# A whole output tile ahead of the pairs, squares a step later and joins ahead of the low halves, in a hybrid pooling and attention layer on one core

## The chip, the core and the metric

The kernel runs on one core of a Trainium2 chip. The engines are TensorE (PE, its weight loads PEld), VectorE (DVE), ScalarE (ACT), GpSimd (POOL) and SyncE (SP). SP and POOL only issue transfers in the part that matters here. The metric is the device time of one execution in microseconds (us). The time before is a median of 853.5 us.

## The reference, cut to what matters

The layer takes 512 prompt rows and 8 sample rows (520 columns once turned), projects them, runs pooling and attention branches, and ends with an output projection, a residual and a final RMS norm. The change touches only this last part.

```
def merge_out(pm, gp, a, ga, w_out, dtype):
    mix = jnp.concatenate([pm * silu(gp), a * silu(ga)], axis=-1)      # 520 x 2048
    return jnp.einsum('btm,md->btd', mix, w_out)                        # w_out is 2048 x 2048
...
xp = xp + merge_out(...)
y_prompt = rms_norm(xp, final_norm_g)     # y * rsqrt(mean(y*y) + 1e-6) * g
```

## The kernel before, in words

All products are made of three fp32 matmuls: each operand is split in a high half (ScalarE copies it to `..._hi`) and a low half (VectorE subtracts: `..._lo`), and TensorE sums high by high, high by low and low by high. A column block of `w_out`, 128 wide, is an output tile `d`, 16 of them. Each takes 16 blocks of 128 rows of `w_out` (`k`).

The work is written as a list of steps, the same for each engine, and each engine runs its own part of every step in turn. 144 steps belong to the input projection. Those of the output are counted here from 0 (`n`).

- **Whole tiles.** Tiles 0, 1 and 2 are woven: steps 0 to 8 run their three chunks (6, 5 and 5 `k`) in turn, into the banks `pj[0]`, `pj[1]` and `ps_s`/`ps_o`. A chunk is loaded three steps ahead by SP (`load_chunk`) into one of three slots of `w_raw`, split two steps ahead (`split_hi`, line 1130, and `split_lo`, line 1559), and used by `chunk` (line 864).
- **Pairs.** Tiles 3 to 12 go in five pairs ("duos"), six steps each, numbered k = 0 to 5 here. A pair uses sums of halves of the weights and of the inputs so that its first eight `k` take seven products instead of eight. Its units are w11, s1, s2, s3, w12, s4, w22 (12 matmuls each) and std1x, std1y, std2x, std2y for the other eight `k` (24 each): 180 matmuls of 260 columns, all on line 1022. The std2y unit of a pair runs in step 0 of the next. Weights go through a ring of six places in `w_hi`, `w_lo` and `parts` (`unit_hi_of`, line 1354, `unit_lo_of`, lines 2080 and 2084); VectorE makes the weight sums s1 to s4 (`weight_sum`, line 2105).
- **Joins.** ScalarE takes snapshots of partial sums from PSUM (`snapshot`, line 1366, and `take_c21`, line 1372). VectorE adds a bank and a snapshot (`meet`, line 2112, "join" here), three in step 5 and one in step 1 of the next pair, and turns the finished tile (`turn_both`, lines 2119 and 2120). w11 of the next pair waits for the second join of step 5.
- **The trip of a tile.** After the turn, POOL stores the tile to a scratch in DRAM in four transfers (`send_tile`, line 1532), SP loads it back as rows (`load_rows`, line 637), VectorE adds the residual (`add_res`, lines 2018 and 2021), ScalarE squares it for the norm (`y_square`, line 1325, five instructions with their accumulator reads) and VectorE scales it by `g` (`scale_y`, lines 2030 and 2031). SP then loads the residual of tile d + 3 into the freed buffer (`load_res`, line 644).
- **Input sums for the pairs.** VectorE makes them in steps 2 to 7 (`whole_x`, `form_sums`, `form_lo_of`), ScalarE their high halves in steps 5 and 6.
- **The end.** Tile 13 (`SOLO`) is a whole tile after the pairs. Tiles 14 and 15 are last: columns 256 to 519 as halves (`half_chunk`, line 890), taken by `half_evict` (line 1314) and turned on TensorE (`turn_half`), then rows 0 to 255 directly (`row_chunk`, line 901). `half_add`, `half_square`, `root` and `scale_last` finish the norm and SP stores the rows.

In ScalarE's list of a step the order is snapshots of `duo_early`, high halves, snapshots of `duo_late`, then squares. In VectorE's list it is

```
if IN_CHUNKS + SEVEN - 2 <= step < IN_CHUNKS + AFTER:
    for p, u in units_ahead(step):
        unit_lo_of(p, u)
    duo_sums(step)
if duo_at(step):
    duo_out(*duo_at(step))
```

Of the kernel before, what the change touches and what calls it, by code (L numbers as in the profile page):

```python
# [28 lines left out]
KT = D_MODEL // P  # L29
# [29 lines left out]
SEVEN = WOVEN * 3  # L59
DUO_STEPS = 6  # L60
AFTER = SEVEN + DUOS * DUO_STEPS
SOLO = WOVEN + 2 * DUOS
OUT_SEQ = tuple((d, c) for c in range(3) for d in range(WOVEN)) + tuple(
    (d, c) for d in range(SOLO, KT) for c in range(3))
# [76 lines left out]
def layer_step(nc, x_prompt, x_sample, state_pool, cache_k, cache_v, norm_g, w_in, pool_w,  # L141
               pool_scale, w_out, final_g, consts, y_prompt, y_sample, pool_state_p, k_win_p,
               v_win_p, pool_state_s, k_new, v_new):
    with ExitStack() as ctx:
# [299 lines left out]
        def split_ahead(step):  # L444

            n = step - IN_CHUNKS
            if n <= SEVEN - 3 or n >= AFTER + 1:
                return (chunk_at(step + 2),) if n < OUT_CHUNKS - 2 else ()
            return {AFTER - 1: (chunk_at(step + 1),),
                    AFTER: (chunk_at(step + 1), chunk_at(step + 2))}.get(n, ())  # L450
# [24 lines left out]
        TAIL = IN_CHUNKS + SEVEN + 3  # L475
# [20 lines left out]
        def w_both(c):  # L496

            lo, hi = TAIL_CHUNKS[c]
            if c == 0:
                flat = [a.rearrange("p j x -> p (j x)") for a in (pt_hi, pt_lo)]  # L500
            elif c == 1:
                flat = [a[:, 0:2].rearrange("p s k x -> p (s k x)") for a in (w_hi, w_lo)]
            else:
                flat = [a.rearrange("p j x -> p (j x)") for a in (v_hl, pooled_lo)]
            return tuple(a[:, 0:HP * (hi - lo)].rearrange("p (k x) -> p k x", k=hi - lo)
                         for a in flat)

        def out_bank(d):

            return (ps_s, ps_o) if d in (2, SOLO) else pj[d % 2 if d < 2 else (d + 1) % 2]  # L510
# [5 lines left out]
        def done_at(d):  # L516

            if d < WOVEN:
                return IN_CHUNKS + OUT_N[d, 2]
            if d >= SOLO:  # L520
                return IN_CHUNKS + 3 * d + 2
            p, second = divmod(d - WOVEN, 2)
            return IN_CHUNKS + SEVEN + DUO_STEPS * p + (7 if second else 4)

        def rows_at(d):

            return done_at(d) + (5 if d < WOVEN else 4)

        def added_at(d):

            return done_at(d) + (7 if d < WOVEN else 5)

        def duo_banks(p):

            a, b = (pj[0][0], pj[1][0]) if p % 2 == 0 else (pj[1][0], pj[0][0])
            return {"a": a, "b": b, "c": pj[0][1], "d": pj[1][1]}
# [14 lines left out]
        def _(sp):  # L551

            def load_chunk(n):
# [102 lines left out]
            def load_duo(p, what):  # L656

                m1, m2 = WOVEN + 2 * p, WOVEN + 2 * p + 1
# [28 lines left out]
            for step in range(STEPS):  # L687
                if step + 3 < IN_CHUNKS + SEVEN:
                    load_chunk(step + 3)
                elif step == IN_CHUNKS + AFTER - 2:  # L690
                    load_chunk(IN_CHUNKS + SEVEN)
                elif step == IN_CHUNKS + AFTER - 1:
                    load_chunk(IN_CHUNKS + SEVEN + 1)
                    load_chunk(IN_CHUNKS + SEVEN + 2)
                elif step == IN_CHUNKS + AFTER:
                    load_chunk(IN_CHUNKS + SEVEN + 3)
# [40 lines left out]
                if n == 4:  # L737
                    load_duo(0, "c")
                if n == 5:
# [3 lines left out]
                if n == 7:  # L743
# [3 lines left out]
                if n == 10:  # L747
# [3 lines left out]
                if n in (11, 12):  # L751
                    load_res(n - 10)
                if n >= 0:
# [3 lines left out]
                    for e in range(3, KT):  # L757
                        if step == added_at(e - 3) + 2:
                            sp.wait_ge(y_scaled, e - 2)
                            load_res(e)  # L760
            for e in range(3, KT):
                if added_at(e - 3) + 2 >= STEPS:
# [34 lines left out]
        def _(pe):  # L797
# [28 lines left out]
            def chunk(n):  # L826
# [6 lines left out]
                else:  # L833
# [6 lines left out]
                    elif c == 0:  # L840
                        pe.wait_ge(yt_done, WOVEN)
# [200 lines left out]
            def duo_step(p, k):  # L1042

                if k == 0:
                    if p < DUOS:
                        pe.wait_ge(*((yt_done, 1) if p == 0 else (met, 4 * p - 2)))
# [10 lines left out]
                if k == 2:  # L1057
                    pe.wait_ge(*((yt_done, 2) if p == 0 else (c21_out, p)))
# [53 lines left out]
        def _(act):  # L1112
            def split_hi(n):
# [4 lines left out]
                if n >= TAIL and c == 1:  # L1118
                    act.wait_ge(w_used, TAIL)
                elif n == IN_CHUNKS + SEVEN:  # L1120
                    act.wait_ge(unit_used, RING_N[DUOS - 1, "w12"] + 1)
                elif n == IN_CHUNKS + SEVEN + 1:
                    act.wait_ge(unit_used, RING_N[DUOS - 1, "s4"] + 1)
                elif n == IN_CHUNKS + SEVEN + 2:
                    act.wait_ge(unit_used, RING_N[DUOS - 1, "w22"] + 1)
                elif n == TAIL:
                    act.wait_ge(unit_used, len(RING_SEQ))
# [240 lines left out]
            def take_c21(p):  # L1368

                act.wait_ge(unit_used, RING_N[p, "std2y"] + 1)  # L1370
                act.wait_ge(yt_done, WOVEN + 2 * p + 1)
# [19 lines left out]
            for step in range(STEPS):  # L1391
# [41 lines left out]
                if n == 5:  # L1433
                    form_hi_of("nt1")
                    form_hi_of("t3")
                if n == 6:
# [103 lines left out]
        def _(dve):  # L1540
# [467 lines left out]
            def add_res(d):  # L2008
# [8 lines left out]
                op = ALU.subtract if WOVEN <= d < SOLO and (d - WOVEN) % 2 == 1 else ALU.add  # L2017
# [113 lines left out]
            def duo_out(p, k):  # L2131
# [4 lines left out]
                if k == 2 and p > 0:  # L2136
                    dve.wait_ge(met, 4 * p)
                    dve.wait_ge(c21_out, p)
                    turn_both(WOVEN + 2 * p - 1)
                if k == 5 and p < DUOS:  # L2140
# [5 lines left out]
                    turn_both(WOVEN + 2 * p)  # L2146

            for step in range(STEPS):
                for pr, j, p in due(step):
                    early(pr, j, p)  # L2150
                if step > 0:
                    for m in split_ahead(step):
                        split_lo(m)
                if IN_CHUNKS + SEVEN - 2 <= step < IN_CHUNKS + AFTER:
# [3 lines left out]
                if duo_at(step):  # L2158
                    duo_out(*duo_at(step))
                for d in range(KT - 2):  # L2160
                    if step == done_at(d) + 1 and (d < WOVEN or d >= SOLO):
# [28 lines left out]
                if n in (2, 3):  # L2190
                    whole_x(n - 2)
                if n in (4, 5):
                    form_sums(n - 4)
                if n == 6:
                    form_lo_of("nt1")
                    form_lo_of("t3")
                if n == 7:
                    form_lo_of("nt2")
                    form_lo_of("t4")
                for d in range(KT - 2):  # L2200
                    if step == added_at(d) + 1:
# [120 lines left out]
```

## Time and profile before

| | us |
|---|---|
| median of three runs | 853.5 |
| lowest, highest | 852.5, 856.26 |
| the profiled execution's own time | 853.96 |
| its span, first to last instruction | 852.2 |
| mean granted TensorE clock, share of full speed | 0.988 |

The profiled execution is 1.8 us longer than its span and 0.5 us above the median. TensorE is busy 830.2 us of the span. The page's slices show it at nine tenths or more of each slice except in three of the last seven of forty, and the input projection (to about 655 us) is no part of the change. What follows reads the stretch from 680 us to the end.

### The profile page before, as it was taken

Reading aid. Unit: us, or ns where it says so; the run is one execution under the profiler, and the core shown is the slowest. Engines: PE = TensorE matmul, PEld = TensorE weight load, DVE = VectorE, ACT = ScalarE, POOL = GpSimd, SP = SyncE. Lnnn points to the kernel's source line nnn. Section 1 sums busy time; section 2 is a strip of 40 time slices with the busy share of each in tenths; the row PEclk is TensorE's granted clock in tenths of the full one; section 3 lists DMA queues with packets and bytes.
Section 4 is the critical chain, followed back from the end, with each engine's and each line's share of the span. In section 5 each row is a group of like instructions: output and inputs, shape, how many; then the busy total and the mean of one; then the engine's idle time right before and its main releaser. Section 6 shows DMA issues by size and latency. Waiting matters only on the chain.

```text
span 852.2 us, 17454 instructions
## 1 busy us (share of the span) xinstructions
PE 830.2 (97%) x6765; PEld 823.3 (97%) x6765; DVE 608.0 (71%) x1305; ACT 395.2 (46%) x875; POOL 98.3 (12%) x172
## 2 busy tenths in 40 slices
PE   9999999999999999999999999999999998999985
PEld 8999999999999999999999999999999988999975
DVE  5646884797579568757975796688788967767445
ACT  5745535423543454255435434643463545555443
POOL 2001000201010001002000101010001032222220
PEclk9999999999999999999999999999999998999988
DMA  8566347537544752564366347534768375565645
GB/s 286 151 169 163 91 121 176 131 105 177 147 110 117 193 141 78 167 173 111 93 173 165 98 134 196 150 89 129 182 187 299 96 219 157 157 181 154 198 117 202
DMA packets 247307, 131.69 MB, mean 155 GB/s; under 512 B 40864, under 2 KB 239968, under 8 KB 247200
## 3 DMA queue, kind: packets, MB, share of 16 engines
q1 hardware_dynamic: 239928, 119.17, 51.3%
q0 software_dynamic: 7296, 11.40, 4.3%
q8 instruction: 54, 0.88, 0.5%
q14 instruction: 29, 0.24, 0.1%
HBM read 110.32 MB, written 19.10 MB: 152 GB/s over the span
## 4 chain that ended last, share of the span: by engine, by line
PE 86%; DVE 5%; DMA 3%; ACT 2%; issue 1%; SPq 1%; POOL 0%; DVEq 0%; ACTq 0%
PE pj L864 66%; PE pj L1022 9%; PE ps_t L908 2%; PE ps_o L952 1%; PE ps_s L923 1%; PE ps_s L921 1%; DMA arena<-in_x_prompt 1%; PE ps_o L950 1%; ACT arena L1325 1%; PE ps_s L969 1%; PE ps_t L969 1%; PE pj L890 1%; DVE w_lo L2084 1%; PE ps_o L864 0%; PE ps_s L864 0%
## 5 line engine op out<-in xcount | busy, mean ns | idle before, releaser
L864 PE MATMUL pj<-mov_hi,w_hi 128*128 128x260 f32 (+1 forms) x1600 | 328.6, 287 | 0.3 <-DVE mov_lo L1580 0.3
L864 PE MATMUL pj<-mov_hi,w_lo 128*128 128x260 f32 (+1 forms) x1600 | 322.1, 283 | 0.0
L864 PE MATMUL pj<-mov_lo,w_hi 128*128 128x260 f32 (+1 forms) x1600 | 321.3, 282 | 0.0
L864 PEld LDWEIGHTS pj<-mov_hi,w_hi 128*128 128x128 f32 x1600 | 246.4, 189 | 0.9 <-issue 0.7
L864 PEld LDWEIGHTS pj<-mov_lo,w_hi 128*128 128x128 f32 x1600 | 246.4, 188 | 0.0
L864 PEld LDWEIGHTS pj<-mov_hi,w_lo 128*128 128x128 f32 x1600 | 246.4, 188 | 0.0
L1130 ACT ACTIVATE w_hi<-w_raw 128x640 fp32r<-128x640 f32 (+1 forms) x157 | 121.4, 773 | 209.4 <-PE pj L864 176.7
L1559 DVE TENSOR_TENSOR w_lo<-w_raw,w_hi 128x640 fp32r<-128x640 f32 (+1 forms) x157 | 136.0, 866 | 63.3 <-ACT w_hi L1130 63.0
L1190 ACT ACTIVATE parts<-ps_t 128x128 fp32r<-128x128 f32 (+1 forms) x64 | 26.2, 436 | 80.4 <-PE ps_t L908 78.5
L1650 DVE TENSOR_TENSOR parts<-ps_t,parts 128x128 fp32r<-128x128 f32 (+1 forms) x64 | 29.7, 485 | 45.8 <-ACT parts L1190 45.6
L1532 POOL DMA_DIRECT2D y_scratch<-arena x56 | 37.5, 677 | 120.6 <-DVE arena L2120 95.1
L1022 PE MATMUL pj<-mov_hi,w_hi 128*128 128x260 f32 x144 | 41.8, 290 | 5.4 <-DVE arena L2112 2.8
L1597 DVE SCALAR_TENSOR_TENSOR arena<-pj,rstd_bc 128x260 f32<-128x260 f32 (+2 forms) x104 | 36.9, 399 | 13.0 <-PE pj L864 11.2
L1174 ACT ACTIVATE arena<-arena,stat 128x128 f32<-128x128 f32 (+1 forms) x64 | 35.7, 558 | 17.4 <-DVE stat L1636 16.8
L1022 PE MATMUL pj<-mov_hi,w_lo 128*128 128x260 f32 x144 | 41.5, 288 | 0.0
L1022 PE MATMUL pj<-mov_lo,w_hi 128*128 128x260 f32 x144 | 41.5, 288 | 0.0
L1636 DVE CUSTOM_DVE_ANT_0 arena<-ps_s,arena 128x128 f32<-128x128 f32 (+1 forms) x64 | 29.7, 482 | 16.4 <-PE ps_s L923 16.4
L1182 ACT ACTIVATE arena<-arena,stat 128x128 f32<-128x128 f32 (+1 forms) x64 | 34.2, 558 | 14.7 <-DVE stat L1644 14.6
L1325 ACT ACTIVATE arena<-arena 128x128 f32<-128x128 f32 (+1 forms) x70 | 21.7, 310 | 34.0 <-DVE arena L2021 32.2
L1022 PEld LDWEIGHTS pj<-mov_hi,w_hi 128*128 128x128 f32 x144 | 27.9, 193 | 6.2 <-DVE arena L2112 3.3
L1490 POOL DMA_DIRECT2D out<-arena x8 | 4.5, 568 | 243.4 <-DMA arena<-arena 243.4
L1022 PE MATMUL pj<-mov_hi,parts 128*128 128x260 f32 x152 | 30.2, 291 | 0.1
(271 smaller groups left out, 1331.2 us busy)
## 6 DMA issues: line engine op xcount, KB each, us to landing
w_raw<-in_w_in SPq DMA_DIRECT2D x96, 320.0 KB, 3.6
w_raw<-in_w_in SPq DMA_DIRECT2D x48, 384.0 KB, 3.8
arena<-in_cache_k_win SPq DMA_DIRECT2D x16, 384.0 KB
arena<-in_cache_v_win SPq DMA_DIRECT2D x16, 384.0 KB
w_raw<-in_w_out SPq DMA_DIRECT2D x26, 192.0 KB, 3.4
arena<-in_cache_k_win SPq DMA_DIRECT2D x8, 512.0 KB
arena<-in_cache_v_win SPq DMA_DIRECT2D x8, 512.0 KB
arena<-in_x_prompt SPq DMA_DIRECT2D x16, 256.0 KB
```

The costliest lines, as they stand in the source:

```text
L864: mm = pe.matmul(dst[h][:, 0:own.stop - own.start], w, m[:, k, own], start=(k == 0 and i == 0), stop=(c == 2 and k == KT - 1 and i == 2))
L1022: mm = pe.matmul(dst, w[:, own], m(k), start=(at in first and k == 0 and i == 0), stop=(at in last and k == KQ - 1 and i == 2), skip_group ...
L1130: act.activation(w_at(n)[0][:, 0:hi - lo, :], w_raw[:, n % SLOTS, 0:hi - lo, :], ACT.Copy).then_inc(w_hi_done, 1)
L1174: act.activation(pb_, pb_, ACT.Exp, scale=-1.0, bias=nmax[:, i:i + 1], accum_out=den[:, i:i + 1]).then_inc(exped, 1)
L1182: a = act.activation(pb_, pb_, ACT.Copy, scale=rden[:, i:i + 1])
L1190: a = act.activation(pt_hi[:, 0:i + 1, P * i:P * i + P], ps_t[:, at:at + P * (i + 1)].rearrange("p (j x) -> p j x", j=i + 1), ACT.Copy)
L1325: act.activation(sq_junk[0:n, :], src, ACT.Square, accum_out=ss_y[0:n, t, d:d + 1]).then_inc(y_squared, 1)
L1532: pool.dma_start(rows[:, :, own], y_sq[d % 3][own, :].rearrange("p (c x) -> p c x", x=SQ)).then_inc(y_st[d % 3], 16)
L1559: dve.tensor_tensor(to_lo[:, 0:hi - lo, :], w_raw[:, n % SLOTS, 0:hi - lo, :], to_hi[:, 0:hi - lo, :].bitcast(F32), ALU.subtract).then_inc ...
L1597: o = dve.scalar_tensor_tensor(out=dst, in0=pj[a][h][:, c0:c1], scalar=scale, in1=rstd_bc[:, HT * h + c0:HT * h + c1], op0=ALU.mult, op1=A ...
L1636: dve.tensor_tensor_reduce(out=pbuf[r % 2][:, at:at + n], in0=ps_s[:, at:at + n], in1=nbias[:, SEQ - n:SEQ], scale=1.0, scalar=3e38, op0=A ...
L1650: o = dve.tensor_tensor(pt_lo[blk], ps_t[:, at:at + P * (i + 1)].rearrange("p (j x) -> p j x", j=i + 1), pt_hi[blk].bitcast(F32), ALU.subt ...
```

## The change

Tile 3 becomes a whole tile and runs in steps 9 to 11, right after the woven ones, into bank `pj[0]`. The five pairs now make tiles 4 to 13 in steps 12 to 41, and nothing whole is left after them: the last six chunks (tiles 14 and 15) follow at once, and their weights go to places of `parts` that the first pair units leave. The number of matmuls, of split and of stored elements is the same.

```
-SEVEN = WOVEN * 3
+FIRST = WOVEN + 1
+SEVEN = FIRST * 3
...
 OUT_SEQ = tuple((d, c) for c in range(3) for d in range(WOVEN)) + tuple(
-    (d, c) for d in range(SOLO, KT) for c in range(3))
+    (d, c) for d in (WOVEN, KT - 2, KT - 1) for c in range(3))
...
-        TAIL = IN_CHUNKS + SEVEN + 3
+        TAIL = IN_CHUNKS + SEVEN
...
         def rows_at(d):
-            return done_at(d) + (5 if d < WOVEN else 4)
+            return min(done_at(d) + (6 if d < FIRST else 4), STEPS - 2)
         def added_at(d):
-            return done_at(d) + (7 if d < WOVEN else 5)
+            return min(done_at(d) + (8 if d < FIRST else 6), STEPS - 1)
+        def squared_at(d):
+            return min(added_at(d) + 1, STEPS - 1)
+        def scaled_at(d):
+            return min(squared_at(d) + 1, STEPS - 1)
...
-                if n == IN_CHUNKS + SEVEN:
-                    sp.wait_ge(unit_lo, RING_N[DUOS - 1, "std2x"] + 1)
-                elif n == IN_CHUNKS + SEVEN + 1:
-                    sp.wait_ge(unit_lo, RING_N[DUOS - 1, "std2y"] + 1)
+                if TAIL <= n < TAIL + SLOTS:
+                    last = ("std2x", "std2y", "s4")[n - TAIL]
+                    sp.wait_ge(unit_lo, RING_N[DUOS - 1, last] + 1)
...
                 elif step == IN_CHUNKS + AFTER - 2:
-                    load_chunk(IN_CHUNKS + SEVEN)
+                    load_chunk(TAIL)
+                    load_chunk(TAIL + 2)
                 elif step == IN_CHUNKS + AFTER - 1:
-                    load_chunk(IN_CHUNKS + SEVEN + 1)
-                    load_chunk(IN_CHUNKS + SEVEN + 2)
+                    load_chunk(TAIL + 1)
...
-                if n >= TAIL and c == 1:
-                    act.wait_ge(w_used, TAIL)
...
+                if n >= TAIL:
+                    act.wait_ge(unit_used, RING_N[DUOS - 1, "s4" if c == 1 else "s3"] + 1)
...
                 for d in range(KT - 2):
-                    if step == added_at(d):
+                    if step == squared_at(d):
                         y_square(d)
...
+                if duo_at(step):
+                    duo_out(*duo_at(step))
                 if IN_CHUNKS + SEVEN - 2 <= step < IN_CHUNKS + AFTER:
                     for p, u in units_ahead(step):
                         unit_lo_of(p, u)
                     duo_sums(step)
-                if duo_at(step):
-                    duo_out(*duo_at(step))
...
-                if n in (2, 3):
-                    whole_x(n - 2)
+                if n in (3, 4):
+                    whole_x(n - 3)
```

The input sums move one step later, their halves two. Of a pair's two tiles, the first is added in step 4 and squared in step 5 (before: both in step 3), the second added in step 1 and squared in step 2 (before: both in step 0).

ScalarE in a pair in the middle, before, from step 3 to step 1 of the next: `L1325` are squares, `tab<-pj` is the snapshot s3, `rstd_bc<-pj` the snapshot w11, `L1372` is `take_c21`, `L1354` are high halves.

```order
L1325 ACTIVATE arena<-arena 128x128 x4
L1325 ACTIVATE arena<-arena 8x128
L1366 ACTIVATE tab<-pj 128x260
L1354 ACTIVATE w_hi<-tab 128x512
L1354 ACTIVATE w_hi<-w_raw 128x512 x2
L1354 ACTIVATE parts<-w_raw 128x512 x2
L1366 ACTIVATE rstd_bc<-pj 128x260
L1325 ACTIVATE arena<-arena 128x128 x4
L1325 ACTIVATE arena<-arena 8x128
L1372 ACTIVATE arena<-pj 128x260
```

The same engine and place in the changed kernel, where every line number of ScalarE is 5 lower:

```order
L1361 ACTIVATE tab<-pj 128x260
L1349 ACTIVATE w_hi<-tab 128x512
L1349 ACTIVATE w_hi<-w_raw 128x512 x2
L1320 ACTIVATE arena<-arena 128x128 x4
L1320 ACTIVATE arena<-arena 8x128
L1349 ACTIVATE parts<-w_raw 128x512 x2
L1361 ACTIVATE rstd_bc<-pj 128x260
L1367 ACTIVATE arena<-pj 128x260
```

Squares no longer stand ahead of the snapshot s3 or of `take_c21`; they stand behind the high halves of step 5 (and, not shown, of step 2).

VectorE before, in the steps 4 and 5 of a pair: `w_raw<-tab,extra` is the sum s1 of the next pair, `L2030` and `L2031` scale a tile, then the low half and the sum, then the joins (`L2112`) and the turn.

```order
L2084 TENSOR_TENSOR w_lo<-tab,w_hi 128x512
L2080 SCALAR_TENSOR_TENSOR w_lo<-w_raw,w_hi 128x512
L2105 TENSOR_TENSOR w_raw<-tab,extra 128x512
L2030 TENSOR_TENSOR arena<-arena 128x4x128
L2031 TENSOR_TENSOR arena<-arena 8x128
L2084 TENSOR_TENSOR w_lo<-w_raw,w_hi 128x512
L2105 TENSOR_TENSOR w_raw<-w_raw,tab 128x512
L2112 TENSOR_TENSOR tab<-rstd_bc,tab 128x260
L2112 TENSOR_TENSOR arena<-pj,rstd_bc 128x260
```

The same engine and place in the changed kernel; `L2013` and `L2016` are `add_res`:

```order
L2079 TENSOR_TENSOR w_lo<-tab,w_hi 128x512
L2075 SCALAR_TENSOR_TENSOR w_lo<-w_raw,w_hi 128x512
L2100 TENSOR_TENSOR w_raw<-tab,extra 128x512
L2013 TENSOR_TENSOR arena<-arena 128x4x128
L2016 TENSOR_TENSOR arena<-arena 8x128
L2107 TENSOR_TENSOR tab<-rstd_bc,tab 128x260
L2107 TENSOR_TENSOR arena<-pj,rstd_bc 128x260
L2107 TENSOR_TENSOR arena<-pj,extra 128x260
L2114 STREAM_TRANSPOSE arena<-arena 128x512
L2115 STREAM_TRANSPOSE arena<-arena 128x32
L2079 TENSOR_TENSOR w_lo<-w_raw,w_hi 128x512
```

The low half of s1 and the sum s2 now follow the joins and the turn, and an `add_res` stands where the scaling stood.

ScalarE at the end, before, from the first square behind the chunks to the second taking (`L1314` is `half_evict`):

```order
L1130 ACTIVATE parts<-w_raw 128x4x128
L1325 ACTIVATE arena<-arena 128x128 x4
L1325 ACTIVATE arena<-arena 8x128
L1314 ACTIVATE arena<-pj 128x264
L1325 ACTIVATE arena<-arena 128x128 x4
L1325 ACTIVATE arena<-arena 8x128
L1314 ACTIVATE arena<-pj 128x264
```

The same engine and place in the changed kernel:

```order
L1125 ACTIVATE parts<-w_raw 128x4x128
L1309 ACTIVATE arena<-pj 128x264
L1320 ACTIVATE arena<-arena 128x128 x4
L1320 ACTIVATE arena<-arena 8x128
L1320 ACTIVATE arena<-arena 128x128 x4
L1320 ACTIVATE arena<-arena 8x128
L1309 ACTIVATE arena<-pj 128x264
```

The taking of tile 14 now stands ahead of both last squares (tiles 12 and 13), that of tile 15 behind both.

## Rows read from the trace of the kernel before

**Rows 1.** The page's first part: busy time of each engine and its share.

```profile
PE 830.2 (97%) x6765; PEld 823.3 (97%) x6765; DVE 608.0 (71%) x1305; ACT 395.2 (46%) x875; POOL 98.3 (12%) x172
```

**Rows 2.** Windows of TensorE: stretch, length, busy (count), granted clock, DMA share, GB/s.

```profile
684.00:688.00 4.00, 3.20 (x25) 1.00 0.27 56
701.00:710.00 9.00, 6.21 (x39) 0.81 0.51 132
713.00:720.00 7.00, 4.83 (x28) 0.76 0.67 184
819.00:824.00 5.00, 0.89 (x8) 0.81 0.34 96
824.00:829.00 5.00, 5.00 (x24) 0.51 0.24 68
```

**Rows 3.** Timeline of TensorE: start, length, instruction: first matmul of pairs, tile 13, tile 14.

```profile
681.84 0.28 PE L1022 MATMUL pj<-mov_hi,parts 128*128 128x260 f32 x1
800.07 0.28 PE L864 MATMUL ps_s<-mov_hi,w_hi 128*128 128x256 f32 x1
811.59 0.28 PE L890 MATMUL pj<-mov_hi,parts 128*128 128x264 f32 x1
```

**Rows 4.** The chain in order of time from 728 us: start, length, what.

```profile
727.93 41.49 PE pj L1022 x346
```

**Rows 5.** Timeline in the first pair: VectorE and ScalarE; brackets: idle before, releaser.

```profile
698.38 0.69 DVE L2105 TENSOR_TENSOR w_raw<-tab,extra 128x512 f32<-128x512 f32 x1 [1.34 <-DMA extra<-in_w_out]
698.98 0.68 DVE L2018 TENSOR_TENSOR arena<-arena 128x512 f32<-128x512 f32 x1
699.89 0.31 ACT L1325 ACTIVATE arena<-arena 128x128 f32<-128x128 f32 x1 [3.67 <-DVE arena L2021]
702.59 0.69 DVE L2084 TENSOR_TENSOR parts<-w_raw,parts 128x512 fp32r<-128x512 f32 x1 [2.73 <-ACT parts L1354]
704.26 0.42 DVE L2112 TENSOR_TENSOR arena<-pj,rstd_bc 128x260 f32<-128x260 f32 x1
```

**Rows 6.** The same timelines, in the third and fourth pair.

```profile
744.36 0.69 DVE L2018 TENSOR_TENSOR arena<-arena 128x512 f32<-128x512 f32 x1 [0.80 <-DMA arena<-y_scratch]
745.28 0.31 ACT L1325 ACTIVATE arena<-arena 128x128 f32<-128x128 f32 x1 [2.50 <-DVE arena L2021]
748.24 0.69 DVE L2084 TENSOR_TENSOR w_lo<-tab,w_hi 128x512 fp32r<-128x512 f32 x1 [3.00 <-ACT w_hi L1354]
766.58 0.69 DVE L2018 TENSOR_TENSOR arena<-arena 128x512 f32<-128x512 f32 x1 [0.79 <-DMA arena<-y_scratch]
```

**Rows 7.** The same at the end, with POOL, SP and TensorE.

```profile
802.18 0.83 ACT L1130 ACTIVATE parts<-w_raw 128x768 fp32r<-128x768 f32 x1
809.12 0.96 DVE L1559 TENSOR_TENSOR w_lo<-w_raw,w_hi 128x768 fp32r<-128x768 f32 x1 [4.00 <-ACT w_hi L1130]
810.00 0.70 DVE L2119 STREAM_TRANSPOSE arena<-arena 128x512 f32<-128x512 f32 x1
811.09 5.34 POOL L1532 DMA_DIRECT2D y_scratch<-arena x8 [12.09 <-DVE arena L2120]
816.27 0.38 SPq L637 DMA_DIRECT2D arena<-y_scratch  x1
820.47 0.69 DVE L2018 TENSOR_TENSOR arena<-arena 128x512 f32<-128x512 f32 x1 [2.13 <-DMA arena<-y_scratch]
823.43 0.36 ACT L1314 ACTIVATE arena<-pj 128x264 f32<-128x264 f32 x1
823.85 0.69 PE L908 MATMUL ps_t<-tab,arena 128*128 128x128 f32 x2 [4.11 <-ACT arena L1314]
824.63 0.39 SPq L644 DMA_DIRECT2D arena<-in_x_prompt  x1
832.82 0.42 DVE L2210 TENSOR_TENSOR arena<-ps_s,arena 128x256 f32<-128x256 f32 x1 [5.40 <-PE ps_o L908]
841.75 0.28 PE L901 MATMUL pj<-parts,mov_hi 128*128 128x256 f32 x1
842.71 0.48 DVE L2220 TENSOR_TENSOR arena<-pj,arena 128x128 f32<-128x128 f32 x2
```

**Rows 8.** The page's DMA issues: destination<-source, queue, operation, count, KB each, median us to landing.

```profile
w_raw<-in_w_in SPq DMA_DIRECT2D x48, 384.0 KB, 3.8
w_raw<-in_w_out SPq DMA_DIRECT2D x26, 192.0 KB, 3.4
```

More of the change, by code:

```diff
@@ L448, in split_ahead @@
                 return (chunk_at(step + 2),) if n < OUT_CHUNKS - 2 else ()
-            return {AFTER - 1: (chunk_at(step + 1),),
-                    AFTER: (chunk_at(step + 1), chunk_at(step + 2))}.get(n, ())
+            return {AFTER - 1: (TAIL,), AFTER: (TAIL + 1, TAIL + 2)}.get(n, ())
         def units_ahead(step):
@@ L498, in w_both @@
             lo, hi = TAIL_CHUNKS[c]
-            if c == 0:
-                flat = [a.rearrange("p j x -> p (j x)") for a in (pt_hi, pt_lo)]
-            elif c == 1:
+            if c == 1:
                 flat = [a[:, 0:2].rearrange("p s k x -> p (s k x)") for a in (w_hi, w_lo)]
             else:
-                flat = [a.rearrange("p j x -> p (j x)") for a in (v_hl, pooled_lo)]
+                at = 0 if c == 0 else HP * 6
+                flat = [parts[:, at + h:at + h + HP * 6] for h in (0, len(FORMS) * WING)]
             return tuple(a[:, 0:HP * (hi - lo)].rearrange("p (k x) -> p k x", k=hi - lo)
@@ L736, in _ @@
                     load_split(i)
-                if n == 4:
+                if n == SEVEN - 5:
                     load_duo(0, "c")
-                if n == 5:
+                if n == SEVEN - 4:
                     sp.wait_ge(own_done, PAIRS)
@@ L750, in _ @@
                     load_res(0)
-                if n in (11, 12):
-                    load_res(n - 10)
+                if n in (SEVEN, SEVEN + 1):
+                    load_res(n - SEVEN + 1)
                 if n >= 0:
@@ L757, in _ @@
                     for e in range(3, KT):
-                        if step == added_at(e - 3) + 2:
+                        if step == scaled_at(e - 3) + 1:
                             sp.wait_ge(y_scaled, e - 2)
@@ L2016, in add_res @@
                 cols = slice(P * d, P * d + P)
-                op = ALU.subtract if WOVEN <= d < SOLO and (d - WOVEN) % 2 == 1 else ALU.add
+                op = ALU.subtract if d >= FIRST and (d - FIRST) % 2 == 1 else ALU.add
                 dve.tensor_tensor(y[:, :, cols],
@@ L2157, in _ @@
                     duo_sums(step)
-                if duo_at(step):
-                    duo_out(*duo_at(step))
                 for d in range(KT - 2):
-                    if step == done_at(d) + 1 and (d < WOVEN or d >= SOLO):
+                    if step == done_at(d) + 1 and d < FIRST:
                         turn_out(d)
@@ L2200, in _ @@
                 for d in range(KT - 2):
-                    if step == added_at(d) + 1:
+                    if step == scaled_at(d):
                         scale_y(d)
```

55 lines of the change are left out of this document (22 added, 33 removed).

## The prediction

> **What bounds the kernel now.** Start with the page's first part: TensorE is busy for 97% of the span and no other engine for more than 71% [rows 1], so only TensorE's idle or slow time can be won, plus what lies behind its last matmul. The windows of TensorE in the changed stretch come next. It is short of work in four places [rows 2]: a little at 684 us, then 2.8 us idle from 701 and 2.2 us from 713, both followed by a granted clock of half speed, and at 819 us, where 4.1 us idle is again followed by half speed.
>
> How much the pairs lose is best read over their whole length. They run from the first matmul of w11 at 681.84 to the first of tile 13 at 800.07 [rows 3], 118.2 us for 5 x 180 = 900 matmuls. In the dense stretch of the chain 346 matmuls take 41.49 us [rows 4], 0.1199 each, so 900 need 107.9. **The pairs lose 10.3 us.** The windows agree: idle 0.8 + 2.8 + 2.2 = 5.8, slow clock (1 - 0.81) x 9 + (1 - 0.76) x 7 = 3.4, together 9.2 [rows 2]; the rest is what the windows hide, since a matmul is 0.28 long and one starts every 0.12 [rows 3, 4], so 0.16 of each gap counts as busy.
>
> Why they lose it is read from the timelines of VectorE and ScalarE. VectorE's sum s1 waits 1.34 us for a transfer at 698.38, the residual add stands behind it, ScalarE can square only from 699.89, and the high half that VectorE wants for s1 stands behind those squares: VectorE idles 2.73 us before 702.59. The join that lets the next w11 go is behind all this, at 704.26 [rows 5]. So TensorE waits for a chain that is late because the first pair starts with its helpers already behind. Later pairs show a second, milder thing: squares at 745.28 (behind an add that waited 0.80 us for its rows) hold the snapshot s3 and the halves behind it, so VectorE idles 3.00 us before 748.24. The adds follow one another at 744.36 and 766.58, 22.2 us apart [rows 6], though 180 matmuls need only 21.6. TensorE, coming late out of the first two pairs, hardly feels this loop; it would on time.
>
> At the end, VectorE's low half waits 4.00 us before 809.12, because its high half waits for tile 13's second chunk on TensorE; the turn of tile 12 stands behind it at 810.00. Its trip ends in an add at 820.47, squares, the taking at 823.43 and TensorE's turning at 823.85 [rows 7]. That is the 4.1 us.
>
> **Part by part.** *The whole tile ahead of the pairs.* It costs TensorE nothing net, 96 matmuls either way (811.59 - 800.07 = 11.5 us [rows 3]). For the helpers it is cover: in those 11.5 us VectorE gets three low halves of at most 0.96 and a turn of about 0.9 (as one of 0.70 plus a short one) [rows 7], 3.8 in all, and ScalarE three high halves, under 3. So VectorE gains 7.7 us on TensorE before the first pair, ScalarE over 8. The three waits that the first two pairs showed sum to 5.8 us idle, and these are lateness that adds up along one chain; 7.7 covers it with 1.9 to spare. The input sums one step later and their halves two steps later stay ahead: a step is 3.6 us or more, and the first use moved three steps. SP's loads for the first pairs and three residual loads, which now crowd the transfers (one of them is what s1 waited for at 698.38), move with the steps and get the same 11.5 us. That the moved loads cost anything is bounded by the 1.34 us of that wait, below the cover, so I take nothing.
>
> *Squares a step later.* Off ScalarE's path from unit s3 to the next join come five squares of about 2.1 us (699.89 to the high half behind them, [rows 5]). New positions are behind high halves that TensorE needs only two units later. From the end of s3, snapshot, two high halves, low half, sum s1, add and two joins are 0.4 + 1.1 + 0.7 + 0.7 + 0.9 + 0.8 = 4.6 us (durations as in rows 5 to 7), while TensorE has w12, s4, w22 and std2x ahead of w11, 60 matmuls or 7.2 us. Slack 2.6 us. What is late next is nothing in a pair; the y rows now have a full step more, and the trip of 10.5 us (810.00 to 820.47, [rows 7]) fits in the 18 us between turn and add. The loop of 22.2 us opens.
>
> *Joins ahead of the low halves.* The join c waits for s4 on TensorE, and s1's low half of the next pair is queued behind three joins and a turn, about 1.9 us. TensorE wants it after w22, std2x, w11 and std2y, 72 matmuls or 8.6 us after s4. Cost nothing, with 6.7 us of cover.
>
> So the pairs should run at 21.6 us each and **end at 681.84 + 11.5 + 107.9 = 801.3** against 811.6 for the same work. Up to 0.3 us of small waits may remain.
>
> *The end.* The halves of tile 14 now start at 801.3. Their chunks are ready: the first's slot is free when the last std2x low half is, some 12 us earlier, the second's and third's some 8 us earlier. What is left is the last tile's trip, which has lost the cover of tile 13:
> - std2y ends at 801.3, snapshot 0.4, high half 0.85, low half 0.9, join 0.35, add 0.9, low half 0.9: turn of tile 13 starts at about 805.6;
> - add at 805.6 + 10.5 = 816.1 (810.00 to 820.47), end 817.0;
> - squares and taking: 823.85 - 821.35 = 2.5 from the end of the add to the turning, so 819.5 [rows 7]; the add of 820.47 ends 0.9 later.
>
> TensorE meanwhile does 48 + 18 matmuls, a turning that is ready in time, 30, and 18 of the first row chunk: 114 x 0.1199 + 0.4 = 14.1, to 815.4. It **waits 4.1 us again**, until 819.5, and falls to half speed as at 824 (lost (1 - 0.51) x 5 = 2.4). Then 78 matmuls: 0.7 + 9.4 + 2.4, last one at 832.0. Before, the last was at 841.75 + 0.3 [rows 7]. So TensorE ends 10.1 us sooner at least; before, VectorE picked it up 0.7 us late (842.71), which it need not now. On VectorE, the residual load of tile 15 goes out after the scaling of tile 12 at about 817.9 (before: 824.63) and lands within the 4.2 us that rows take (816.27 to 820.47), 822.1; `half_add` then, against 832.82, is 10.7 sooner, and its last row add at 832.0 too. Both paths meet at 832.0, where 842.71 was. **Gain 10.7 us.**
>
> A row and the skill differ here. Between the end of POOL's first four issues (811.09 + 2.67 = 813.76) and SP's load at 816.27 lie 2.5 us [rows 7]. The Trainium skill, "DMA: Bandwidth & Descriptors", section "Anatomy of one DMA — SWDGE (gpsimd) path", gives about 2.0 us fixed plus bytes / 436e3, which for 68 KB is an estimate of 2.2 us. By it the trip would be 0.3 us shorter and the gain 11.0.
>
> The sum is made on the span of 852.2, which becomes 841.5; the profiled run is 1.8 longer than its span and 0.5 above the median, so against the median of 853.5 the forecast is **842.8 us**.
>
> **Rivals.**
> - *The end is worse than counted.* The second store of two took longer to be picked up than the first, and the rows' load ranges over a microsecond; with a second stretch of half speed like that from 824 to 829 (2.4) and the trip 1.2 longer, the time is 844.5 to 846.5. For it: everything there is serial now. Against: only about 1 us of it is unpriced.
> - *The loop of 22.2 us stays.* If SP's queue, not the squares, sets it, each pair costs 0.6 us more: 842.8 + 3.1 = 845.9. For: the add waits for rows in both pairs [rows 6]. Against: the add now stands a step later.
> - *Half of the first stall stays.* If the first pairs are late for transfers and not for VectorE, the 2.8 us idle with its 1.7 of slow clock returns: 847.3.
> - *The end is better.* If the last tile's trip is short by 1.5 us, 841.3; less is barred by VectorE's own list behind `half_add`.
> - *The change doesn't do what it says:* the pairs are dense but the end takes all back. The half tiles use a chunk in 18 matmuls, 2.2 us, where tile 13 took 4.3. With three slots, a load (3.8 us, [rows 8]), a high half (0.83) and a low half (0.96, [rows 7]) give one chunk in 1.9 us, just faster. If loads went one at a time, three chunks at 5.6 us each would cost 3 x 3.4 = 10.2: 853.0, no change.
> - *Slower.* The joins ahead of the low halves turn into the bound: a join waits for TensorE (s4), the low half behind it, TensorE for that. It starts to cost once the low half comes more than 8.6 us after s4 instead of 1.9, and outweighs the gain at 2.1 us more per pair (10.7 / 5). With 3.5 us per pair the time is 842.8 + 17.5 = 860.3. Nothing in the rows is near it.
>
> **How the numbers follow.** Forecast 842.8, own range 841.3 to 844.5: 0.58. Worse end 0.14, loop 0.10, half a stall 0.07, better end 0.05; no change 0.03; slower 0.03. A measurement of this kernel can tell about 0.5% (4.3 us) from no change: faster means under 849.2. The first five cases are there, 0.94; same 0.03; slower 0.03. The range takes the forecast's own and reaches over the worse end and the loop: 841.0 to 846.8, leaving out the half stall and what lies beyond, and part of the better end.
>
> **What would show it.** In the windows of the changed kernel, TensorE without idle time and at full clock from 655 us to about 815 us; the first pair's matmuls from 693.4 and tile 14's from 801.3. In the timelines, no squares between s3's snapshot and the next join, adds 21.6 us apart. At the end, one wait of TensorE of about 4 us before the turning for tile 15, caused by ScalarE's taking behind the squares of tile 13, then half speed. The prediction is wrong if TensorE waits in `duo_step` for a low half, a join or the bank of tile 3, if the half tiles wait for chunks, or if the last wait is far from 4 us.

## The result, and the profile after

The changed kernel takes **840.24 us** (median of 4 runs, 839.13 to 842.67) against 853.4 of the kernel before: a ratio of 0.9844, 95% interval 0.9812 to 0.9876. That is 13.2 us less where 10.7 were forecast. The forecast of 842.8 was 2.6 us too slow, and the fast end of its range, 841.0, was too slow by 0.8; the ratio's interval, which is 837.4 to 842.8 us, reaches over that end of the range. The profiled run has a span of 838.1 us where the sum came to 841.5.

The windows of TensorE (stretch, length, busy (count), granted clock, DMA share, GB/s), after, against [rows 2]:

```profile
684.00:688.00 4.00, 4.00 (x36) 1.00 0.44 99
701.00:710.00 9.00, 9.00 (x77) 1.00 0.58 166
713.00:720.00 7.00, 7.00 (x61) 1.00 0.70 189
815.00:820.00 5.00, 2.95 (x15) 0.73 0.23 66
820.00:825.00 5.00, 5.00 (x41) 0.93 0.27 100
```

The three places of the pairs have closed. The chain of waits after (start, length, what) shows the pairs in one piece, and then the end:

```profile
681.52 11.53 PE pj L867 x96
693.05 107.75 PE pj L1025 x900
...
804.93 0.62 DVE arena L2114
...
808.39 2.13 DMA y_scratch<-arena
810.53 0.36 SPq L640
810.94 2.71 DMA arena<-y_scratch
813.67 0.69 DVE arena L2013
...
814.56 0.60 DVE arena L2025
...
815.39 0.37 SPq L647
815.81 0.41 SPq L649
816.26 2.92 DMA arena<-in_final_norm_g
819.28 0.42 DVE arena L2205
```

900 matmuls of the pairs take 107.75 us, where 107.9 was the forecast. Behind them TensorE no longer stands in the chain that ended last. The chain goes by the turn of tile 13 (804.93), its stores, its rows' load, its add (813.67), the scaling of tile 12 (814.56), the three transfers of the residual load of tile 15 (the last is the row of `g`) and `half_add` (819.28).

TensorE's own wait at the end is there, at the place that was forecast, but half as long:

```profile
816.64 0.36 ACT L1309 ACTIVATE arena<-pj 128x264 f32<-128x264 f32 x1
817.05 0.53 PE L911 MATMUL ps_s<-tab,arena 128*128 128x128 f32 x2 [2.17 <-ACT arena L1309]
828.08 0.28 PE L904 MATMUL pj<-parts,mov_hi 128*128 128x256 f32 x1
829.18 0.48 DVE L2215 TENSOR_TENSOR arena<-pj,arena 128x128 f32<-128x128 f32 x2
```

Since runs reach the changed stretch at 659.5 to 661.8 us, kernels are compared below by three lengths, read from TensorE's timeline. P runs from the matmul right behind the last product of the mixing (660.15 before, 659.67 after) to the first of tile 14: the same matmuls in every kernel, 140.95 us at their best. T runs from there to TensorE's last matmul, E from there to the span's end. All three come from the one profiled run of each kernel. Of the 14.1 us between the spans before and after, P has 10.5, T 2.7, E 0.4 and the earlier arrival 0.5.

| kernel | median us | ratio (95% interval) | P | T | E |
|---|---|---|---|---|---|
| before | 853.4 | 1 | 151.4 | 30.2 | 10.4 |
| after | 840.24 | 0.9844 (0.9812 to 0.9876) | 141.0 | 27.4 | 10.0 |
| e3_tile_only | 847.06 | 0.9907 (0.9886 to 0.9928) | 147.6 | 27.0 | 10.6 |
| e1_squares_back | 850.95 | 0.9953 (0.9939 to 0.9968) | 150.8 | 26.6 | 10.6 |
| e2_joins_back | 840.91 | 0.9839 (0.9814 to 0.9864) | 141.0 | 27.4 | 9.2 |
| e4_no_tile | 841.85 | 0.9851 (0.9829 to 0.9874) | 142.5 | 26.2 | 10.6 |
| n1_squares_only | 841.92 | 0.9853 (0.9836 to 0.9871) | 142.2 | 27.2 | 10.3 |
| n2_adds_back | 843.64 | 0.9877 (0.9862 to 0.9892) | 141.0 | 29.3 | 10.4 |
| n3_same_step | 846.78 | 0.9907 (0.9890 to 0.9925) | 142.0 | 29.6 | 10.7 |
| t1_store_traffic | 841.26 | 0.9850 (0.9836 to 0.9865) | 141.0 | 27.0 | 10.3 |
| v1_take_first | 839.89 | 0.9840 (0.9827 to 0.9854) | 141.0 | 23.6 | 12.7 |
| v2_scale_first | 838.98 | 0.9830 (0.9816 to 0.9843) | 141.0 | 26.0 | 10.4 |
| v3_both | 837.49 | 0.9808 (0.9795 to 0.9822) | 141.0 | 23.6 | 11.7 |

The kernel before, measured again beside each group of runs, had medians of 853.4 (after), 854.79 (e), 854.42 (n) and 853.66 (t and v). So a difference of about 1 us between medians of different groups says nothing; the ratios take it out.

### The profile page after: what moved, and what is told of

Read it like the earlier page. It is cut to its first block, busy times and chain, and to the rows that moved or that the text cites. A ratio compares the mean times of both kernels' runs of the same rounds, so it can differ in the third digit from the quotient of the medians.

```text
span 838.1 us, 17458 instructions
## 1 busy us (share of the span) xinstructions
PE 822.6 (98%) x6765; PEld 817.0 (97%) x6765; DVE 608.5 (73%) x1305; ACT 395.8 (47%) x875; POOL 98.3 (12%) x172
## 4 chain that ended last, share of the span: by engine, by line
PE 94%; DMA 2%; DVE 1%; SPq 1%; ACT 1%; issue 0%; POOL 0%; DVEq 0%; ACTq 0%
PE pj L867 70%; PE pj L1025 13%; PE ps_t L911 2%; PE ps_o L955 1%; PE ps_s L926 1%; PE ps_s L924 1%; DMA arena<-in_x_prompt 1%; PE ps_o L953 1%; PE ps_o L867 1%; PE ps_t L972 1%; PE ps_s L972 1%; PE ps_s L867 1%; PE ps_m L911 0%; DMA arena<-in_final_norm_g 0%; DMA arena<-y_scratch 0%
## 5 line engine op out<-in xcount | busy, mean ns | idle before, releaser
L867 PE MATMUL pj<-mov_hi,w_hi 128*128 128x260 f32 (+1 forms) x1632 | 335.0, 287 | 0.6 <-DVE w_lo L1582 0.6
L867 PE MATMUL pj<-mov_hi,w_lo 128*128 128x260 f32 (+1 forms) x1632 | 328.6, 283 | 0.0
L867 PE MATMUL pj<-mov_lo,w_hi 128*128 128x260 f32 (+1 forms) x1632 | 327.8, 282 | 0.0
L867 PEld LDWEIGHTS pj<-mov_hi,w_hi 128*128 128x128 f32 x1632 | 251.3, 189 | 1.0 <-issue 0.7
L867 PEld LDWEIGHTS pj<-mov_lo,w_hi 128*128 128x128 f32 x1632 | 251.4, 188 | 0.0
L867 PEld LDWEIGHTS pj<-mov_hi,w_lo 128*128 128x128 f32 x1632 | 251.3, 188 | 0.0
L1185 ACT ACTIVATE parts<-ps_t 128x128 fp32r<-128x128 f32 (+1 forms) x64 | 26.2, 435 | 79.4 <-PE ps_t L911 77.2
L1592 DVE SCALAR_TENSOR_TENSOR arena<-pj,rstd_bc 128x260 f32<-128x260 f32 (+2 forms) x104 | 36.9, 400 | 12.2 <-PE pj L867 10.3
L1485 POOL DMA_DIRECT2D out<-arena x8 | 4.5, 567 | 244.4 <-DMA arena<-arena 244.4
L1705 DVE TENSOR_TENSOR arena<-arena 128x128 f32<-128x128 f32 (+3 forms) x48 | 28.8, 601 | 1.6
L1501 POOL DMA_DIRECT2D out<-arena x32 | 16.3, 510 | 100.4 <-DVE arena L1944 100.4
```

The source lines that it names most:

```text
L867: mm = pe.matmul(dst[h][:, 0:own.stop - own.start], w, m[:, k, own], start=(k == 0 and i == 0), stop=(c == 2 and k == KT - 1 and i == 2))
L1185: a = act.activation(pt_hi[:, 0:i + 1, P * i:P * i + P], ps_t[:, at:at + P * (i + 1)].rearrange("p (j x) -> p j x", j=i + 1), ACT.Copy)
L1592: o = dve.scalar_tensor_tensor(out=dst, in0=pj[a][h][:, c0:c1], scalar=scale, in1=rstd_bc[:, HT * h + c0:HT * h + c1], op0=ALU.mult, op1=A ...
L1705: o = dve.tensor_tensor(out, vv[:, P * to:P * (to + n)], vv[:, P * other:P * (other + n)], ALU.add)
```

## The experiments: which part closed the waits in the pairs

**The tile alone**, both smaller parts undone:

```diff
-            return min(done_at(d) + (6 if d < FIRST else 4), STEPS - 2)
+            return min(done_at(d) + (5 if d < FIRST else 4), STEPS - 2)
...
-            return min(done_at(d) + (8 if d < FIRST else 6), STEPS - 1)
+            return min(done_at(d) + (7 if d < FIRST else 5), STEPS - 1)
...
-            return min(added_at(d) + 1, STEPS - 1)
+            return added_at(d)
...
-                if duo_at(step):
-                    duo_out(*duo_at(step))
                 if IN_CHUNKS + SEVEN - 2 <= step < IN_CHUNKS + AFTER:
...
+                if duo_at(step):
+                    duo_out(*duo_at(step))
```

> The changed kernel with both smaller parts undone: only the whole tile stands ahead of the pairs. Theory of the prediction: the three waits of the first two pairs go (10.3 us less 3.3 for the loop of 22.2 us), 843.5. Rival: the tile alone does everything, 840.2 to 841. Second rival: the halves need both, and one of the first stalls comes back with its slow clock, 845 to 848.

Measured: 847.06, which is the second rival, and P = 147.6. The tile by itself is worth 3.8 of the 10.5 us. The largest stall is not covered: it has only moved, from ahead of the second pair to ahead of unit w22 of the first, which wants the taking of s3. In the kernel before it was this one:

```profile
704.74 0.39 PE L1022 MATMUL pj<-mov_hi,w_hi 128*128 128x260 f32 x1 [2.79 <-DVE arena L2112]
```

Timelines of VectorE, ScalarE and TensorE of the tile-only kernel:

```profile
697.74 0.68 DVE L2013 TENSOR_TENSOR arena<-arena 128x512 f32<-128x512 f32 x1
698.64 0.31 ACT L1320 ACTIVATE arena<-arena 128x128 f32<-128x128 f32 x1 [1.84 <-DVE arena L2016]
700.96 0.62 ACT L1349 ACTIVATE parts<-w_raw 128x512 fp32r<-128x512 f32 x1
701.61 0.69 DVE L2079 TENSOR_TENSOR parts<-w_raw,parts 128x512 fp32r<-128x512 f32 x1 [3.00 <-ACT parts L1349]
703.42 0.68 DVE L2013 TENSOR_TENSOR arena<-arena 128x512 f32<-128x512 f32 x1
704.33 0.31 ACT L1320 ACTIVATE arena<-arena 128x128 f32<-128x128 f32 x1 [1.72 <-DVE arena L2016]
706.38 0.62 ACT L1349 ACTIVATE w_hi<-w_raw 128x512 fp32r<-128x512 f32 x1
707.02 0.69 DVE L2075 SCALAR_TENSOR_TENSOR w_lo<-w_raw,w_hi 128x512 fp32r<-128x512 f32 x1 [1.92 <-ACT w_hi L1349]
707.63 0.68 DVE L2013 TENSOR_TENSOR arena<-arena 128x512 f32<-128x512 f32 x1
708.54 0.31 ACT L1320 ACTIVATE arena<-arena 128x128 f32<-128x128 f32 x1 [1.55 <-DVE arena L2016]
710.59 0.36 ACT L1361 ACTIVATE tab<-pj 128x260 f32<-128x260 f32 x1
711.00 0.51 PE L1025 MATMUL pj<-parts,w_hi 128*128 128x260 f32 x2 [3.13 <-ACT tab L1361]
```

Read it as a ring. VectorE's add of tile 0 (L2013) releases ScalarE's five squares (L1320, 2 us); the high half of the next step (L1349) stands behind them; VectorE's low half waits for it; the next tile's add stands behind the low half. A round takes 5.7 and 4.2 us, and both engines wait in it. Three tiles are added in a row here, and the taking of s3 (L1361), which TensorE wants, stands behind the third. The helpers had been in time: in the changed kernel and here alike, ScalarE waits 3.53 us for TensorE's w11 before its first taking, at 694.5 and 695.0. That the tile gave them no lead is read so: the next things in their lists are takings of what TensorE has yet to compute.

**The two smaller parts without the tile**: the kernel before with the changed kernel's steps of adds and squares and its order of the joins (the lines that the diff above takes out).

> The kernel before with the two smaller parts alone: adds a step and squares two steps later, joins ahead of the low halves, tile 13 still behind the pairs. Theory of the prediction: the first pair starts with its helpers late, so the waits of 2.8 and 2.2 us and the slow clock behind them stay: 851 to 853.5. Rival: VectorE's wait of 2.73 us at 702.59 was for squares, and the join behind it was what TensorE waited for, so these two parts take away most of the 10 us by themselves: 843 to 846.

Measured: 841.85. The theory of the prediction falls: without the tile P is 142.5, and all that is left of the waits are two of 0.6 us (by the starts of the matmuls) at 685 and 687 us. Beside the two smaller parts the tile is worth 1.5 us of P. The windows that lost most, at 701 and 713 us, close without the tile.

**The smaller parts one by one**: joins back (the last piece of that diff on the changed kernel), and squares back (its other pieces).

> The changed kernel with the joins behind the low halves and the sums again in each step of VectorE's list; the tile ahead and the late squares stay. Theory of the prediction: the joins have 6.7 us of cover either way, so the pairs stay at 107.7 us and the time at 840.2 within 1. Rival: a join behind a low half that waits for its high half holds the next w11 or std2x as at 704.26 in the kernel before, 0.6 us in each of 5 pairs: 843.2.

Measured: 840.91, P the same to a hundredth. The joins ahead of the low halves bring nothing that shows.

> The changed kernel with the adds and squares of the output rows back at their old steps (adds 5 or 7 steps after a tile's last unit, squares in the same step); the tile ahead of the pairs and the joins ahead of the low halves stay. Theory of the prediction: the squares in ScalarE's list set a loop of 22.2 us per pair, so the pairs take 5 x 22.2 = 111 instead of 107.7 us and the time is 840.2 + 3.3 = 843.5. Rival: the helpers come out of the extra tile some 7.7 us ahead, and a loop of 22.2 us eats only 0.6 of that per pair, 3 us in all, so TensorE never feels it and the time stays 840.2 within 1. Slower than 843.5 would mean that the squares also hold the first pair.

Measured: 850.95, slower than either theory had, and 3.9 us slower than the tile alone, from which it differs only in that the joins stand ahead of the low halves. It has the same stall in the first pair (3.29 us by the starts of the matmuls), and then one in each later pair. ScalarE, VectorE and TensorE of this kernel:

```profile
744.35 0.27 DVE L2016 TENSOR_TENSOR arena<-arena 8x128 f32<-8x128 f32 x1
744.66 0.31 ACT L1320 ACTIVATE arena<-arena 128x128 f32<-128x128 f32 x1 [1.96 <-DVE arena L2016]
746.71 0.36 ACT L1367 ACTIVATE arena<-pj 128x260 f32<-128x260 f32 x1
747.10 0.43 DVE L2107 TENSOR_TENSOR arena<-pj,tab 128x260 f32<-128x260 f32 x1 [2.48 <-ACT arena L1367]
747.62 0.69 DVE L2079 TENSOR_TENSOR w_lo<-w_raw,w_hi 128x512 fp32r<-128x512 f32 x1
748.47 0.36 PE L1025 MATMUL pj<-mov_hi,w_hi 128*128 128x260 f32 x1 [1.18 <-issue]
```

The join (L2107) waits 2.48 us for a taking (L1367) that stands behind squares, and the low half that TensorE starts with at 748.47 is now behind the join. This is the "slower" rival of the prediction in part: a low half stands behind a join. But this join is the one of step 1, which waits for `take_c21` behind squares and not for s4, and the price is smaller: about 1 us in a pair (waits of 0.5, 1.3, 1.7 and 1.1 us), and only while the squares are early.

**The late squares alone**, in the kernel before, and two runs that part "late" into its two steps:

> The kernel before with one part alone: adds a step and squares two steps later; no tile moved, joins behind the low halves. New theory: what TensorE waited for was a ring between two lists. ScalarE's squares stand in the step of VectorE's add and ahead of the next high halves; the next add stands behind the low halves that want these high halves. Each tile added in a row costs a round of 4.2 to 5.7 us where TensorE's step takes 3.6. Squares in a later step break the ring. Then this part alone gives nearly all: pairs at 109 us, 841.5 to 843. Rival: the joins ahead of the low halves do a share of it: 845 to 849.

Measured: 841.92, P = 142.2. One part of three, step numbers alone, gives 9.2 of the 10.5 us in P.

> The changed kernel with the adds back at their old step, the squares one step behind them. The ring's theory: it is the step between add and squares that counts, so the pairs stay dense: 840.2 within 1. Rival: what helps is that the adds wait for no rows any more (0.80 us before), and the ring comes back: 845 or more.

In code: `rows_at` and `added_at` with 5, and 7 or 5; `squared_at` stays `added_at + 1`. Measured: P = 141.0, so the pairs are as dense as with the adds late. The time is 843.64 all the same. T is 1.9 us longer and E 0.4; another 2.1 us of the profiled run is that it reached the stretch later. At the end, the high half of tile 14's second chunk comes at 806.70, so the turn of tile 13 starts 5.7 us behind the first matmul of tile 14 instead of 4.2, and TensorE waits 3.24 us before its last turning. The load of the chunk came last, not the squares ahead: ScalarE idles between them and the high half.

```profile
806.70 0.84 ACT L1125 ACTIVATE w_hi<-w_raw 128x768 fp32r<-128x768 f32 x1 [0.58 <-DMA w_raw<-in_w_out]
```

Here this load stands behind a residual load in SP's queue; in the changed kernel it went out ahead of it.

> The changed kernel with the squares in the step of the add again, both a step later than in the kernel before. The ring's theory: the ring is back, though every add comes later: a wait of about 3 us and a slow clock in the first pair, and the joins ahead of the low halves now wait for the takings behind the squares, about 1 us in every pair: 848 to 851. Rival: the later add is what helps: 840.2 to 841.5.

In code: `squared_at(d)` returns `added_at(d)`, with the late adds. Measured: P = 142.0, where the ring's theory wanted about 150. The span of the profiled run (844.79) is 4.9 us behind the changed kernel's: 2.2 in T, 1.0 in P, 0.7 in E and 1.1 of later arrival. The median of 846.78 is two us more, which the other runs have and no trace shows. So the theory needs a correction. The ring is back (squares behind adds at 702.12, 706.34 and 712.02), but only two of its rounds lie ahead of the taking of s3 instead of three:

```profile
708.38 0.36 ACT L1361 ACTIVATE tab<-pj 128x260 f32<-128x260 f32 x1
708.80 0.51 PE L1025 MATMUL pj<-parts,w_hi 128*128 128x260 f32 x2 [0.32 <-ACT tab L1361]
```

TensorE waits 0.32 us instead of 3.13. These rows show that a round of the ring costs about 4 us and that TensorE has slack for nearly two. The account that fits all runs is that either delay (of the add, or of the squares behind it) takes the third round out from in front of s3 and the squares away from the taking that the join wants. Both delays one by one were run only beside the whole tile and the early joins, not in the kernel before.

## The experiments: the end

The last tile's trip from turn to add was priced at 10.5 us by the kernel before. It takes 8.8 (804.86 to 813.67). The DMA issues (count, KB each, median us to landing) from 809 to 823 us in the kernel before, and of the same stores in the changed kernel:

```profile
y_scratch<-arena POOLq DMA_DIRECT2D x8, 68.0 KB, 3.1
...
w_raw<-in_w_out SPq DMA_DIRECT2D x1, 320.0 KB, 3.1
...
w_raw<-in_w_out SPq DMA_DIRECT2D x1, 192.0 KB, 3.8
w_raw<-in_w_out SPq DMA_DIRECT2D x2, 64.0 KB, 3.0
```

```profile
y_scratch<-arena POOLq DMA_DIRECT2D x4, 68.0 KB, 2.2
```

**Traffic put back.** In the changed kernel:

```diff
+                if d == KT - 3:
+                    sp.wait_ge(unit_used, len(RING_SEQ))
+                    sp.wait_ge(yt_done, KT - 2)
+                    for raw in (raw_a, raw_b, raw_c):
+                        sp.dma_start(raw.rearrange("p (k x) -> p k x", k=4),
+                                     wo[:, 0:4, 0:P]).then_inc(id_in, 16)
                 sp.wait_ge(y_st[d % 3], Y_ST * (d // 3 + 1))
```

> The changed kernel with three more loads of 256 KB each into tiles that nobody reads any more, issued by SP when the turned tile 13 goes to its stores, ahead of SP's wait for these stores. Theory A: the last tile's trip took 10.5 us in the kernel before and 8.8 us now because the stores shared the DMA engines with loads of weights (3.1 us to land against 2.2). Then the four stores land about 1 us later, the add of tile 13 comes at 10 us or more behind its turn, and the time is 1 to 2 us longer, 841.2 to 842.2. Rival B: stores behind one another in POOL's queue made the difference (eight in a row before, four now); then nothing moves, 840.2.

Measured: the stores land in 3.5 us, the rows' load goes out at 811.77, the add of tile 13 comes 9.9 us behind its turn, and TensorE waits 3.23 us:

```profile
806.86 1.33 POOL y_scratch L1533 x2
808.19 3.57 DMA y_scratch<-arena
811.77 0.37 SPq L646
...
814.54 0.69 DVE arena L2019
```

The last DMA of the chain is 3.57 us long instead of 2.13 (the changed kernel's chain, above). Theory A holds for the stores, which explains 1.1 us of the 1.7. From the start of the last store to SP's load of the rows are 3.2 us in the kernel before, 2.1 in the changed one and 3.6 here; from that load to the add 4.2, 3.1 and 2.8. So this run put the stores back in company and not the rows' load, whose share of the trip stays untested. The time, 841.26, is not told apart from the changed kernel's: `half_add` of tile 15 is 1.0 us later, but from it to the span's end are 17.6 us where the changed kernel had 18.8. In the Trainium skill, "DMA: Bandwidth & Descriptors", section "Anatomy of one DMA — SWDGE (gpsimd) path", the fit gives an estimate of 2.2 us for 68 KB; the trace agrees where little else moves (2.2) and not beside other transfers (3.1 and 3.5).

**Two bounds of the end.** Three kernels build on the changed one. The first moves the taking of the last half tile ahead of the squares of tile 13 in ScalarE's list, the second the scaling of tile 12 ahead of the add of tile 13 in VectorE's, and the third does both and lets the half adds pass the scaling of tile 13. The main lines of the third:

```diff
             half_evict(KT - 1)
+            y_square(KT - 3)
...
+            add_res(KT - 3)
             half_add(KT - 2)
             half_add(KT - 1)
             half_square()
+            scale_y(KT - 3)
```

> The changed kernel with one move in ScalarE's list: the taking of the last half tile ahead of the squares of tile 13. TensorE's wait of 2.2 us before the last turning and the slow clock behind it (1.7 us) go, so its last matmul comes about 3.9 us sooner. Theory: the end is VectorE's by now (residual load released by a scaling at 815.09, landed 819.28, then 10 us of work without a gap of note), so the time stays 840.2, at most 0.6 less. Rival: TensorE's end still sets the time: 836.5.

> The changed kernel with one move in VectorE's list: the scaling of tile 12 ahead of the add of tile 13, so that the residual load of tile 15 goes out some 3.4 us sooner. The half add of tile 15 then waits for TensorE's turning and the work ahead of it in the list, 818.1 instead of 819.28. Theory: 1.1 us less on VectorE, but TensorE's last matmul at 828.1 now holds the last row add, so 0.6 less in all: 839.6. Rival: the load was not what VectorE waited for: 840.2.

> Both moves, and the half adds and the half square ahead of the scaling of tile 13, which waits for the last squares. VectorE's sum of squares then starts at about 817.2 instead of 820.79, and TensorE's last matmul comes at about 824.2. Theory: the end has two bounds that lie 0.6 us apart, and only both moves together give the gain: 3.5 us less, 836.7. Rival: the stores of the result or the last squares set the end, under 1 us less.

Measured: 839.89, 838.98 and 837.49. The first takes all waiting from TensorE (T = 23.6, 3.9 less: the wait of 2.2 and 1.7 of slow clock) and gives nothing to the time: E grows from 10.0 to 12.7. So the end of the changed kernel is VectorE's. The second comes out 0.9 us under the first, about as expected, but their intervals overlap, and TensorE kept full speed behind its wait there, which the expectation had not counted. The third gains 2.4 us on the first: its interval, 0.9795 to 0.9822, lies below that of the first, 0.9827 to 0.9854. It is the fastest kernel here, 1.9% under the kernel before. Expected were 3.5 us; what is left is in its chain, where `half_add` still waits for a residual load. That load no longer waits for the add of tile 13, but it follows another in SP's queue:

```profile
812.47 0.43 SPq L647
812.95 0.41 SPq L649
813.40 3.56 DMA arena<-in_final_norm_g
817.05 0.42 DVE arena L2206
```

## Why the prediction was right and wrong

- **Direction and the pairs' length** were right: 107.75 us for 900 matmuls against 107.9, no wait and full clock up to 814.61 us, first matmul of tile 14 at 800.63 against 801.3 (0.5 of the difference is that the run reached the stretch sooner). The adds follow one another at 718.83, 740.37 and 761.92, 21.5 us apart, as said.
- **The step that failed most** is "7.7 covers it with 1.9 to spare", with the sentence behind it that lateness adds up along one chain. It gave the 5.8 us idle time to the tile. The runs give 3.8 us of P to the tile alone, and 9.2 to the late squares alone. A lead of VectorE and ScalarE is lost at the next taking, as far as the 3.53 us wait shows; what delayed them was no starting debt but a ring of rounds, made anew in each step in which add and squares stood together. The rows of the first pair had it in them: the prediction saw the squares ahead of the high half that VectorE awaits for 2.73 us before 702.59 [rows 5], but took them for the tail of a late transfer, and they are one round of the ring. Because the three parts were there together, the error did not show in the sum.
- **The squares' slack and the joins at nothing** were right in the changed kernel (e2_joins_back). The joins are not free in themselves: with early squares they cost 3.2 us of P ahead of the low halves.
- **The loop of 22.2 us** is real but small: in the tile-only kernel the adds at 729.88, 752.11 and 774.26 are 22.2 us apart, and TensorE loses 0.1 to 0.3 us in each of some eight places there, with their smallest parts about 1.7 us in all, not 3.
- **The term of the sum that was mis-sized**, and that put the forecast too slow, is the end: the last tile's trip was priced at 10.5 us and took 8.8. The span came out 3.4 us under the sum: 0.5 from the run's earlier arrival, 0.2 in the pairs, 2.1 between tile 14's first matmul and the last row add (28.6 us against 30.7), and 0.6 behind it (8.9 against 9.5 us). Of the 2.1, 1.7 is the trip, which had its price from the kernel before, where its stores shared the DMA engines with 640 KB of weights and another tile's stores (t1_store_traffic bears that out for the stores; for the rows' load it is not shown); the residual load of tile 15 took 3.9 us and not 4.2. The rival of a better end had this mechanism, with 1.5 us and a chance of 0.05.
- **The wait forecast at 4.1 us** was 2.17, for the same reason, and the slow clock behind it cost 1.7 and not 2.4. By the prediction's own sign ("if the last wait is far from 4 us") this part was wrong. It mattered less than said: VectorE's path was taken to meet TensorE's at 832.0, and in fact ended at 829.18, after TensorE's last matmul at 828.08.

## What to carry to other kernels

Where two engines work through fixed lists and each step has work of the one that waits for the other and stands ahead of what the other wants next, look for the ring and count its rounds up to the next thing that the bound engine waits for; moving one link by a step was worth more here than a whole tile of cover. Don't count on a lead being kept across an instruction that takes what the bound engine has just made. And price a transfer's trip at the traffic that it will have in its new place, not at that of its old one: here the same stores took 2.2 us with little else moving and 3.1 to 3.5 in company.

## What was unexpected of the hardware

Whether TensorE's clock falls behind a wait did not go by the wait's length. After 2.17 us in the changed kernel it was granted half speed for a while, after 3.13 in the tile-only kernel a mean of 0.66 over 5 us, and after only 1.90 in n1_squares_only 0.74 and then 0.58 in two stretches of 2.5 us; after 3.23 us in the kernel with more traffic it kept full speed. Windows of TensorE, changed kernel, then the kernel with traffic:

```profile
817.50:820.00 2.50, 2.50 (x14) 0.50 0.11 31
820.00:822.50 2.50, 2.50 (x20) 0.86 0.00 0
```

```profile
817.00:820.00 3.00, 2.09 (x18) 1.00 0.38 111
820.00:825.00 5.00, 5.00 (x44) 1.00 0.12 44
```

The wait of 2.21 us in v2_scale_first kept full speed too (78 matmuls in 9.5 us). So a term for slow clock behind a wait of two or three microseconds is a chance of some 1.7 us (the price in the changed kernel), and not a fixed price. What decides it, these runs do not show.
